# Hybrid streaming encoder step on 8 cores: stores and loads of x column by column inside the last down projection, weight casts with a marker for each half, and finish steps moved later

## The chip, the cores and the metric

The kernel runs on the 8 cores of one Trainium2 chip, each core on its own share of the streams (2 of the 16 prompt streams, 4 of the 32 sample streams). There is no traffic between cores. The metric is the device time of the slowest core in microseconds, as a median of runs.

## The reference

Two layers, each of them:

```python
x += 0.5 * down(silu(gate(norm(x))) * up(norm(x)))    # w1_*, D_MODEL 1024, D_FF 2816
z  = norm(x) @ w_in                                   # 3072 columns: qa ka va qb kb vb
oa = chunk-band attention (8 heads x 64, 9 chunks of 64 keys, relative bias, QK-norm)
ob = differential attention (4 heads, q/k halves of 64, values of 128, QK-norm, rotary, over the whole past)
x += concat(oa, norm(ob) * (1 - lam_init)) @ w_out
x += 0.5 * down(silu(gate(norm(x))) * up(norm(x)))    # w2_*
```

Outputs are x of the prompt (16 x 2048 rows) and sample streams (32 x 64 rows) and the new keys and values of both attention groups. Inputs and outputs are float32; the kernel multiplies in bfloat16.

## The kernel before

**Groups.** A core works through nine groups of tokens: four of 512 tokens for each of its two prompt streams (`i` is 0 to 3 within a stream, `seq` is 0 or 1), and one of 256 sample tokens. For each group both layers run: `ffn(l, 1)`, `mix(l)`, `ffn(l, 2)`. x of the group stays in SBUF transposed as `xT` (8 columns `dc` of 128 features x 512 tokens). `hT` is the same times the norm's gain, in bfloat16. `BIG` holds 22 tiles of 512 columns: the hidden activations `aT` of an ffn, the padded queries in mix, the staging `xstg` for the output.

**Order.** The program is one list of operations, each added with the tokens that it reads and writes; an operation waits for the last writer (and, if it writes, the readers) of its tokens, and each engine runs its operations in the order in which they were added. So a wait at the head of an engine's list holds everything behind it. DMAs are added to the list of the engine that issues them (SP, or POOL for stores).

**Ring of weights.** 168 weight tiles pass through a ring of 4 slots (`wring`, token `("w", s)`). In the first group every tile is loaded as float32 into borrowed parts of the key and value buffers (`first_load`) and cast into its slot (`first_cast`): the first half by DVE (L438), the second by ACT (L442) or, for w_in and w_out, by POOL (L440). Both halves write the same token. Half of the tiles are then written back in bfloat16 to `wsc` (`first_back`, L444, issued by SP), the others are cast again in the second group and written back then; every later use is a `fetch` (L450) from `wsc`. At the use of tile n the list gets: loads up to tile n+4, casts up to n+2, write-backs up to n+1, fetches up to n+2, in this order.

**ffn** (L542). 22 chunks `fc`: 8 matmuls for gate (L558), 8 for up (L562), then DVE gate x rstd (L568), ACT silu (L571), POOL x rstd (L573), DVE x up (L576). Chunk fc's last DVE step stands ahead of the next chunk's first one on DVE. A pair of chunks (`ft`) uses one gate and one up tile. Then the down projection in two halves of four columns (L582), `down_end` (L588) adds into `xT`, and `norm_feed` (L509, L511) squares and scales the column for the next norm; `norm_flush` (L498) sums the squares on PE.

**Between groups.** `store_y` (L650) transposes all of `xT` back (L657), copies to `xstg` (L661, L664) and stores 2 MB with one POOL DMA; then `load_x` (L629) transposes the next input, prefetched during the last ffn (L639), copies it into `xT` (L643, L646) and feeds the norm. The next gate matmul stands behind all of it.

**mix** (L692). Tables cosT and sinT are loaded by SP at its start, in each layer. A list of 32 jobs for a prompt group (q/k jobs and v jobs) runs as a software pipeline: in each step stages 5, 3, 2, 0, 1 of different jobs. Stage 0 (`Pst`) is the projection (L803 for q/k, L740 for v), stage 1 (`Bst`) the sums of squares (L819) and for group B the rotation matmul (L829), stage 2 (`Rst`) the DVE end of the rotation. The v jobs set the column of ones beside the values with a POOL memset (L751), ahead of ACT's copy of va (L753).

**Attention, prompt.** Group B: tiles of 256 keys, scores (L1032), exp on ACT (L1040), values (L1053), two tiles ahead. After a head's last tile `b_norm_m` (L975 to L979) and `b_combine` (L983) run: DVE adds both halves, squares and reduces (L985 to L991), ACT takes Ln and Exp of 128x4 values (L994, L996), DVE scales (L998). `o_transpose` (L1006) follows 6 tiles later (4 for i = 0). Group A's units follow (L1107, L1112, L1127), then w_out (L936).

## Time and profile before

| what | us |
|---|---|
| runs of the kernel | 7402.94, 7506.07, 7634.82 |
| median | 7506.07 |
| the profiled execution | 7388.71 |
| its span on the slowest core | 7387.7 (all cores 7348.1 to 7387.7) |
| its mean granted TensorE clock by core | 0.958 to 0.962 |

The profiled execution is one run of the program, on core 5. 1 us lies around its span. "Idle before" is the time for which an engine stood still ahead of an instruction, and the name behind the arrow is the instruction that ended the wait.

### The profile page before, as it was taken

The numbers are of one execution on the slowest core, as the hardware profiler recorded it, in microseconds if no ns is written. First come the engines' busy times: TensorE is split into PE (matmuls) and PEld (weight loads), VectorE is DVE, ScalarE is ACT, GpSimd is POOL, SyncE is SP. The second block draws the span as 40 slices with busy tenths as digits, with TensorE's granted clock in tenths as the row PEclk, the third lists the DMA queues.
The fourth block names the chain that finished last, engine by engine and source line by source line (L and its number), as shares of the span: only waits on it lengthen the run. The fifth ranks groups of instructions, "written<-read, shape, count | busy, mean of one in ns | idle before, by whom it ended". The sixth has DMA issues, their size and how long they took to land.

```text
span 7387.7 us, 115930 instructions; the slowest of 8 cores (7348.1 to 7387.7 us)
## 1 busy us (share of the span) xinstructions
PE 6565.3 (89%) x39776; PEld 3502.7 (47%) x39776; DVE 2890.4 (39%) x5156; ACT 2819.4 (38%) x4404; POOL 1504.9 (20%) x1757
## 2 busy tenths in 40 slices
PE   6787888888999998989898999999998989998888
PEld 2433334354444545454444444454545454456666
DVE  3535434343333334333434343333334333333433
ACT  3434335252333426162323233332516162433433
POOL 1212111211212121211212121212120211213332
PEclk9899999999999999999999999999999999998898
DMA  8799673736424242424433443434242424436877
GB/s 242 223 284 292 217 246 114 234 120 219 132 93 142 83 160 72 151 93 141 130 123 126 137 134 104 145 102 144 78 151 73 161 95 127 133 96 223 263 244 243
DMA packets 498890, 1162.09 MB, mean 157 GB/s; under 512 B 42000, under 2 KB 210704, under 8 KB 498320
## 3 DMA queue, kind: packets, MB, share of 16 engines
q1 hardware_dynamic: 480192, 1090.71, 46.7%
q0 software_dynamic: 18128, 63.97, 2.3%
q8 instruction: 335, 5.49, 0.3%
q14 instruction: 235, 1.93, 0.1%
HBM read 1004.57 MB, written 149.95 MB: 156 GB/s over the span
## 4 chain that ended last, share of the span: by engine, by line
PE 59%; DVE 11%; ACT 10%; issue 7%; DMA 6%; POOL 5%; SPq 2%; DVEq 0%; ACTq 0%; POOLq 0%
PE psb L582 14%; PE psb L558 11%; PE psb L562 11%; PE psb L803 6%; POOL tC L573 5%; PE psb L936 3%; PE psb L1032 3%; PE psb L1053 3%; DMA wring<-wsc 3%; ACT tA L571 2%; DVE tA L568 2%; PE psb L740 2%; SPq L270 2%; PE psb L1107 1%; ACT eT L1112 1%
## 5 line engine op out<-in xcount | busy, mean ns | idle before, releaser
L573 POOL TENSOR_TENSOR tC<-tA,rstdT 128x512 f32<-128x512 f32 (+1 forms) x792 | 954.6, 1205 | 4030.3 <-ACT tA L571 4030.3
L558 PE MATMUL psb<-hT,wring 128*128 128x512 bf16 (+1 forms) x6336 | 1446.9, 372 | 100.8 <-ACT wring L442 73.0
L562 PE MATMUL psb<-hT,wring 128*128 128x512 bf16 (+1 forms) x6336 | 1438.5, 370 | 70.8 <-DMA wring<-wsc 42.2
L582 PE MATMUL psb<-BIG,wring 128*128 128x512 bf16 (+1 forms) x6336 | 1325.2, 370 | 80.1 <-DVE BIG L576 43.1
L576 DVE TENSOR_TENSOR BIG<-psb,tC 128x512 bf16<-128x512 f32 (+1 forms) x792 | 524.3, 662 | 1809.8 <-POOL tC L573 1775.8
L571 ACT ACTIVATE tA<-tA 128x512 f32<-128x512 f32 (+1 forms) x792 | 480.9, 607 | 1945.2 <-DVE tA L568 1944.8
L558 PEld LDWEIGHTS psb<-hT,wring 128*128 128x128 bf16 x6336 | 621.1, 99 | 806.7 <-issue 162.1
L582 PEld LDWEIGHTS psb<-BIG,wring 128*128 128x128 bf16 x6336 | 619.8, 98 | 776.6 <-issue 119.0
L562 PEld LDWEIGHTS psb<-hT,wring 128*128 128x128 bf16 x6336 | 618.0, 98 | 771.0 <-issue 116.0
L568 DVE TENSOR_TENSOR tA<-psb,rstdT 128x512 f32<-128x512 f32 (+1 forms) x792 | 516.2, 652 | 182.2 <-ACT rstdT L524 162.7
L1040 ACT ACTIVATE eT<-psb 128x1024 bf16<-128x1024 f32 (+2 forms) x640 | 531.8, 894 | 95.3 <-PE psb L1032 58.8
L803 PE MATMUL psb<-hT,wring 128*128 128x512 bf16 (+1 forms) x2304 | 519.3, 371 | 5.0 <-ACT rstdT L519 4.6
L1032 PE MATMUL psb<-BIG,kbT 128*128 128x512 bf16 (+3 forms) x1280 | 372.1, 367 | 147.7 <-ACT eT L1040 127.8
L588 DVE SCALAR_TENSOR_TENSOR xT<-psb,xT 128x512 f32<-128x512 f32 (+1 forms) x288 | 186.7, 656 | 665.0 <-PE psb L582 664.7
L509 ACT ACTIVATE tq<-xT 128x512 bf16<-128x512 f32 (+1 forms) x216 | 130.9, 608 | 804.6 <-DVE xT L588 627.6
L1053 PE MATMUL psb<-vb,eT 128*128 128x129 bf16 x4352 | 371.6, 229 | 12.2 <-ACT eT L1040 10.9
L1053 PEld LDWEIGHTS psb<-vb,eT 128*128 128x128 bf16 x4352 | 298.3, 102 | 119.6 <-issue 33.3
L803 PEld LDWEIGHTS psb<-hT,wring 128*128 128x128 bf16 x2304 | 226.1, 99 | 228.1 <-issue 19.8
L740 PE MATMUL psb<-wring,hT 128*128 128x256 bf16 (+1 forms) x2304 | 300.1, 275 | 28.9 <-DVE tB L815 28.9
L1112 ACT ACTIVATE eT<-psb 128x1280 bf16<-128x1280 f32 (+4 forms) x256 | 278.5, 1103 | 104.2 <-PE psb L1107 100.9
L936 PE MATMUL psb<-BIG,wring 128*128 128x512 bf16 (+1 forms) x1152 | 275.8, 389 | 0.0
L740 PEld LDWEIGHTS psb<-wring,hT 128*128 128x128 bf16 (+1 forms) x2304 | 226.9, 100 | 89.6 <-issue 37.6
(197 smaller groups left out, 6399.0 us busy)
## 6 DMA issues: line engine op xcount, KB each, us to landing
wring<-wsc SPq DMA_DIRECT2D x1224, 512.0 KB, 3.9
wsc<-wring SPq DMA_DIRECT2D x160, 512.0 KB, 7.1
vb<-w_down SPq DMA_DIRECT2D x65, 512.0 KB, 10.0
vb<-w_gate SPq DMA_DIRECT2D x64, 512.0 KB, 8.7
vb<-w_up SPq DMA_DIRECT2D x64, 512.0 KB, 10.0
kbT<-w_up SPq DMA_DIRECT2D x100, 256.0 KB, 8.8
kbT<-w_gate SPq DMA_DIRECT2D x100, 256.0 KB, 6.5
kbT<-w_down SPq DMA_DIRECT2D x96, 256.0 KB, 8.8
```

Of the source, the lines that this page charges most:

```text
L558: P.add("pe", lambda kc=kc, bg=bg, wg=wg, fl=fl: nc.tensor.matmul(psb[bg][:, 0:T], wg[:, kc, fl * 128:(fl + 1) * 128], hT[:, kc, 0:T], sta ...
L562: P.add("pe", lambda kc=kc, bu=bu, wu=wu, fl=fl: nc.tensor.matmul(psb[bu][:, 0:T], wu[:, kc, fl * 128:(fl + 1) * 128], hT[:, kc, 0:T], sta ...
L568: P.add("dve", lambda bg=bg, ts=ts: nc.vector.tensor_tensor(out=tA[ts][:, 0:T], in0=psb[bg][:, 0:T], in1=rstdT[:, 0:T], op=ALU.mult), ["rs ...
L571: P.add("act", lambda ts=ts: nc.scalar.activation(out=tA[ts][:, 0:T], in_=tA[ts][:, 0:T], func=AF.Silu), [], [("t", ts, "A")])
L573: P.add("pool", lambda ts=ts: nc.gpsimd.tensor_tensor(out=tC[ts][:, 0:T], in0=tA[ts][:, 0:T], in1=rstdT[:, 0:T], op=ALU.mult), [("t", ts, ...
L576: P.add("dve", lambda bu=bu, ts=ts, fc=fc: nc.vector.tensor_tensor(out=aT[:, fc, 0:T], in0=psb[bu][:, 0:T], in1=tC[ts][:, 0:T], op=ALU.mul ...
L582: P.add("pe", lambda: nc.tensor.matmul(psb[ab][:, 0:T], wd[:, fl, dcl * 128:(dcl + 1) * 128], aT[:, fc, 0:T], start=(fc == 0), stop=(fc == ...
L740: P.add("pe", lambda kc=kc: nc.tensor.matmul(psb[b][0:bsz, 0:256], hT[:, kc, tb * bsz:(tb + 1) * bsz], wv[:, kc, :], start=(kc == 0), stop ...
L803: P.add("pe", lambda kc=kc: nc.tensor.matmul(psb[bz][:, 0:T], wv[:, kc, cl * 128:(cl + 1) * 128], hT[:, kc, 0:T], start=(kc == 0), stop=(k ...
L1032: P.add("pe", lambda j=j, u=u, q0=q0, o0=o0, w=w, r=r: nc.tensor.matmul(psall[:, o0:o0 + w], kbT[l][:, h, (j + u) * 128:(j + u + 1) * 128] ...
L1040: P.add("act", lambda: nc.scalar.activation(out=eP[:, es, lo:hi], in_=psall[:, bk * 512 + lo:bk * 512 + hi], func=AF.Exp, scale=0.125), [] ...
L1053: P.add("pe", lambda qt=qt, ob=ob, c=c, u=u: nc.tensor.matmul(psb[ob][:, (qt % 2) * 129:(qt % 2) * 129 + 129], eP[:, es, c:c + 128], vbt[l ...
```

## The change

It has seven parts. (1) The second half of a weight tile gets its own token `("w2", s)`, so ACT's or POOL's cast no longer waits for DVE's; readers wait for both. (2) The write-back to `wsc` is issued by ACT instead of SP. (3) At the end of a group the last down projection takes over the store and the load: `store_chunk` and `load_chunk` handle one column of 128 features; columns 0 to 3 are stored after the first tile of the second half, 0 to 2 loaded after the third and fourth, the others between the last columns' matmuls, 6 and 7 behind them. The output is staged in `hT` and in the first 8 tiles of `BIG`, with one 1 MB store for each half of the features. (4) cosT and sinT are loaded once a group, by POOL at the group's start. (5) The ones beside the values are set only in the first stream, and there for va only in i = 0 and 1. (6) For the q/k jobs of group B, but the first, stages 1, 2 and the row store come one step later, and a step's order is 6, 5, 4, 3, 0, 2, 1. (7) `b_combine` is split: its DVE part writes `tA`, its ACT part and the scaling (`b_finish`) come three tiles later; `o_transpose` follows 6 tiles after the head for every i.

In all matmuls that read a weight tile the token `("w2", ...)` is added to the reads; those lines are left out below.

```diff
@@ -437,21 +437,21 @@
                 if hf == 0:
                     P.add("dve", lambda: nc.vector.tensor_copy(out=dst, in_=buf), tk, [("w", s)])
                 elif name in ("in", "out"):
-                    P.add("pool", lambda: nc.gpsimd.tensor_copy(out=dst, in_=buf), tk, [("w", s)])
+                    P.add("pool", lambda: nc.gpsimd.tensor_copy(out=dst, in_=buf), tk, [("w2", s)])
                 else:
-                    P.add("act", lambda: nc.scalar.copy(out=dst, in_=buf), tk, [("w", s)])
+                    P.add("act", lambda: nc.scalar.copy(out=dst, in_=buf), tk, [("w2", s)])
...
-        dma("sp", wsc[tid][:, 0:nel], wring[:, s, 0:nel], [("w", s)], [("ws", tid)], ("wbk", s))
+        dma("act", wsc[tid][:, 0:nel], wring[:, s, 0:nel], [("w", s), ("w2", s)], [("ws", tid)], ("wbk", s))
...
-        dma("sp", wring[:, s, 0:nel], wsc[tid][:, 0:nel], [("ws", tid)], [("w", s)], ("w", s))
+        dma("sp", wring[:, s, 0:nel], wsc[tid][:, 0:nel], [("ws", tid)], [("w", s), ("w2", s)], ("w", s))
...
@@ -606,11 +606,27 @@
                 for fl in range(nfc):
                     for dcl in range(4):
                         down_mm(4 * t6 + fl, dcl, wd, fl, sd, (4 + dcl) if half == 0 else dcl)
+                if half == 1 and swap is not None:
+                    store_c, load_c = swap
+                    if t6 == 0:
+                        for dc in range(4):
+                            store_c(dc)
+                    for dc in ((), (), (0,), (1, 2))[t6]:
+                        load_c(dc)
             for dcl in range(4):
                 ab = (4 + dcl) if half == 0 else dcl
                 for fc, wd, fl, sd in held:
                     down_mm(fc, dcl, wd, fl, sd, ab)
                 down_end(half, dcl, ab)
+                if half == 1 and swap is not None:
+                    if dcl == 0:
+                        load_c(3)
+                    else:
+                        store_c(3 + dcl)
+                        load_c(3 + dcl)
+        if swap is not None:
+            store_c(7)
+            load_c(7)
 
...
+    def load_chunk(dc, T, b):
+        for tt in range(T // 128):
...
+        norm_flush()
+        if dc % 2 == 0:
+            P.add("act", lambda: nc.scalar.copy(out=xT[:, dc, 0:T], in_=psb[b][:, 0:T]),
+                  [], [PS(b), ("xT", dc)])
+        else:
+            P.add("dve", lambda: nc.vector.tensor_copy(out=xT[:, dc, 0:T], in_=psb[b][:, 0:T]),
+                  [], [PS(b), ("xT", dc)])
+        norm_feed(dc, T, 0, bank=7)
+
     def load_x(T):
+        for dc in range(8):
+            load_chunk(dc, T, rot())
+
+    ystg = [hT[:].rearrange("p c t -> p (c t)").bitcast(F32).rearrange("p (t d) -> p t d", t=4),
+            BIG[:, 0:4096].bitcast(F32).rearrange("p (t d) -> p t d", t=4)]
+    YTOK = [[("hT", c) for c in range(8)], Bk(0, 8)]
+
+    def store_chunk(dc, dst_rows, T, b):
         ntt = T // 128
-        for dc in range(8):
-            b = rot()
-            for tt in range(ntt):
...
-
-    def store_y(dst_rows, T):
-        ntt = T // 128
+        hf, d4 = dc // 4, dc % 4
         for tt in range(ntt):
-            for hf in range(2):
-                b = rot()
-                for d4 in range(4):
-                    dc = hf * 4 + d4
-                    P.add("pe", lambda dc=dc, d4=d4, tt=tt, b=b: nc.tensor.transpose(
-                        psb[b][:, d4 * 128:(d4 + 1) * 128], xT[:, dc, tt * 128:(tt + 1) * 128], ident[:]),
-                        [("xT", dc), "c"], [PS(b)])
-                if hf == 0:
-                    P.add("act", lambda tt=tt, hf=hf, b=b: nc.scalar.copy(
-                        out=xstg[:, tt, hf * 512:(hf + 1) * 512], in_=psb[b][:, :]), [], [PS(b)] + Bk(0, 16))
-                else:
-                    P.add("dve", lambda tt=tt, hf=hf, b=b: nc.vector.tensor_copy(
-                        out=xstg[:, tt, hf * 512:(hf + 1) * 512], in_=psb[b][:, :]), [], [PS(b)] + Bk(0, 16))
-        dma("pool", dst_rows.rearrange("(t p) d -> p t d", p=128), xstg[:, 0:ntt, :], Bk(0, 16), [], "yst")
+            P.add("pe", lambda tt=tt: nc.tensor.transpose(
+                psb[b][:, tt * 128:(tt + 1) * 128], xT[:, dc, tt * 128:(tt + 1) * 128], ident[:]),
+                [("xT", dc), "c"], [PS(b)])
+        out = ystg[hf][:, 0:ntt, d4 * 128:(d4 + 1) * 128]
+        in_ = psb[b][:, 0:T].rearrange("p (t f) -> p t f", t=ntt)
+        wt = [PS(b), ("yst", hf, d4)] + (YTOK[hf] if d4 == 0 else [])
+        if dc % 2 == 0:
+            P.add("act", lambda: nc.scalar.copy(out=out, in_=in_), [], wt)
+        else:
+            P.add("dve", lambda: nc.vector.tensor_copy(out=out, in_=in_), [], wt)
+        if d4 == 3:
+            dma("pool", dst_rows.rearrange("(t p) d -> p t d", p=128)[:, :, hf * 512:(hf + 1) * 512],
+                ystg[hf][:, 0:ntt, :], YTOK[hf] + [("yst", hf, c) for c in range(4)], [], "yst%d" % hf)
+
+    def make_swap(dst_rows, T, Tn):
+        bank = [0]
+
+        def nb():
+            bank[0] += 1
+            return 4 + bank[0] % 3
+        return (lambda dc: store_chunk(dc, dst_rows, T, nb())), (lambda dc: load_chunk(dc, Tn, nb()))
...
@@ -702,11 +731,6 @@
             i = grp["i"]
             sq_ = grp["seq"]
             tok0 = i * 512
-            dma("sp", cosT[:, 0:T], c_cosp[:, i * 512:(i + 1) * 512], [], ["cs"], "cs")
-            dma("sp", sinT[:, 0:T], c_sinp[:, i * 512:(i + 1) * 512], [], ["cs"], "cs")
-        else:
-            dma("sp", cosT[:, 0:T], c_coss[:, 0:T], [], ["cs"], "cs")
-            dma("sp", sinT[:, 0:T], c_sins[:, 0:T], [], ["cs"], "cs")
...
-                if half == 0:
+                if half == 0 and isP and sq_ == 0 and (isBv or i < 2):
                     P.add("pool", lambda: nc.gpsimd.memset(vfull[:, :, dh:dh + 1], 1.0), [], [tok])
                 if isP and not isBv and i < 3:
                     P.add("act", lambda: nc.scalar.activation(
...
-            st_ = {0: Pst, 1: Bst}
+            st_ = {0: Pst, 1 + late: Bst}
             if isB:
-                st_[2] = Rst
+                st_[2 + late] = Rst
             if need_rows:
-                st_[5 if kind == "kb" else 3] = Xst
+                st_[5 + late if kind == "kb" else 3] = Xst
...
         def add_q(kind, c):
-            jobs.append(qk_job(kind, c, nq[0] % 2))
+            late = 1 if kind[1] == "b" and not (kind == "qb" and c == 0) else 0
+            jobs.append(qk_job(kind, c, nq[0] % 2, late))
             nq[0] += 1
...
-        for step in range(nj + 5):
-            for k in (5, 3, 2, 0, 1):
+        for step in range(nj + 6):
+            for k in (6, 5, 4, 3, 0, 2, 1):
...
         def b_combine(h):
-            o4 = tB[0][:, 0:T].rearrange("p (a f) -> p a f", a=4)
+            ob_ = tA[h % 2]
+            OT = ("t", h % 2, "A")
             P.add("dve", lambda: nc.vector.tensor_tensor(
-                out=tB[0][:, 0:T], in0=tB[0][:, 0:T], in1=tB[1][:, 0:T], op=ALU.add),
-                [("t", 1, "B")], [("t", 0, "B")])
+                out=ob_[:, 0:T], in0=tB[0][:, 0:T], in1=tB[1][:, 0:T], op=ALU.add),
+                [("t", 0, "B"), ("t", 1, "B")], [OT])
             P.add("dve", lambda: nc.vector.tensor_tensor(
-                out=tC[0][:, 0:T], in0=tB[0][:, 0:T], in1=tB[0][:, 0:T], op=ALU.mult),
-                [("t", 0, "B")], [("t", 0, "C")])
+                out=tC[0][:, 0:T], in0=ob_[:, 0:T], in1=ob_[:, 0:T], op=ALU.mult),
+                [OT], [("t", 0, "C")])
             P.add("dve", lambda: nc.vector.reduce_sum(
                 out=rz[:, 8:12], in_=tC[0][:, 0:T].rearrange("p (a f) -> p a f", a=4), axis=mybir.AxisListType.X),
                 [("t", 0, "C")], [("rz", 2)])
+
+        def b_finish(h):
+            o4 = tA[h % 2][:, 0:T].rearrange("p (a f) -> p a f", a=4)
             P.add("act", lambda: nc.scalar.activation(out=rz[:, 12:16], in_=rz[:, 8:12], func=AF.Ln,
                                                       scale=1.0 / 128, bias=epsb[:, 0:1]), [("rz", 2), "c"], [("rz", 3)])
             P.add("act", lambda: nc.scalar.activation(out=rz[:, 12:16], in_=rz[:, 12:16], func=AF.Exp, scale=-0.5),
...
-                [("rz", 3), ("t", 0, "B")], [("hT", 4 + c) for c in range(4)])
+                [("rz", 3), ("t", h % 2, "A")], [("hT", 4 + c) for c in range(4)])
...
-                    lag = 4 if i == 0 else 6
-                    deferred.append([idx + lag, o_transpose, (1, h, 6 if lag <= nk // 2 else 4)])
+                    ph = -(-6 // (nk // 2))
+                    deferred.append([idx + 4, b_finish, (h,)])
+                    deferred.append([idx + 6, o_transpose, (1, h, 6 if ph % 2 else 4)])
...
+            if idx == 3:
+                flush(nt + 3)
...
     for gi_, grp in enumerate(groups):
         T = grp["T"]
-        load_x(T)
         if gi_ == 0:
+            load_x(T)
             setup_lam()
             setup_bias()
         nxt = groups[gi_ + 1] if gi_ + 1 < len(groups) else None
+        if grp["kind"] == "p":
+            i_ = grp["i"]
+            dma("pool", cosT[:, 0:T], c_cosp[:, i_ * 512:(i_ + 1) * 512], [], ["cs"], "cs")
+            dma("pool", sinT[:, 0:T], c_sinp[:, i_ * 512:(i_ + 1) * 512], [], ["cs"], "cs")
+        else:
+            dma("pool", cosT[:, 0:T], c_coss[:, 0:T], [], ["cs"], "cs")
+            dma("pool", sinT[:, 0:T], c_sins[:, 0:T], [], ["cs"], "cs")
         for l in range(NL):
             ffn(l, 1, T)
             mix(l, grp)
-            pre = None
+            pre = swap = None
             if l == NL - 1 and nxt is not None:
                 pre = prefetch_x(grp_rows(nxt, xp, xs), nxt["T"])
-            ffn(l, 2, T, pre=pre)
-        store_y(grp_rows(grp, yp, ys), T)
+                swap = make_swap(grp_rows(grp, yp, ys), T, nxt["T"])
+            ffn(l, 2, T, pre=pre, swap=swap)
+        if nxt is None:
+            for dc in range(8):
+                store_chunk(dc, grp_rows(grp, yp, ys), T, rot())
```

## Rows read from the trace of the kernel before

**Rows 1.** The page's first line
```profile
span 7387.7 us, 115930 instructions; the slowest of 8 cores (7348.1 to 7387.7 us)
```

**Rows 2.** Waits of PE, whole span: line waited for, us in total, times, longest
```profile
PE psb L1032 <- ACT eT L1040: 127.8, 131, 2.7
...
PE psb L1127 <- ACT eT L1112: 59.5, 69, 2.5
PE psb L819 <- ACT tq L806: 47.6, 52, 3.7
...
PE psb L562 <- DMA wring<-wsc: 42.2, 26, 3.5
...
PE psb L829 <- ACT tz L809: 21.2, 112, 0.2
```

**Rows 3.** Waits of ACT, whole span, same columns
```profile
ACT wring L442 <- DVE wring L438: 281.7, 92, 17.8
...
ACT rz L994 <- DVE rz L991: 132.0, 64, 3.7
...
ACT va L753 <- POOL va L751: 58.5, 23, 3.1
```

**Rows 4.** Windows, gate/up stretch of groups 1, 2, 3: PE, PEld, DVE, ACT, POOL, PEclk, DMA, GB/s
```profile
354.70:455.10 100.40, 81.16 (x354) 34.61 (x353) 42.01 (x72) 37.33 (x53) 25.32 (x20) 0.97 0.93 276
...
1245.20:1342.80 97.60, 81.47 (x354) 34.90 (x353) 35.78 (x61) 28.07 (x42) 26.56 (x21) 0.95 0.73 226
...
2943.50:3019.70 76.20, 76.20 (x354) 34.53 (x353) 26.34 (x41) 15.86 (x24) 24.62 (x20) 1.00 0.46 146
```

**Rows 5.** Timeline of ACT, then DVE, first group: start, us, instruction, idle before
```profile
112.07 1.05 ACT L442 CAST wring<-vb 128x1024 bf16<-128x1024 f32 x1 [2.89 <-DVE wring L438]
...
114.25 0.63 ACT L571 ACTIVATE tA<-tA 128x512 f32<-128x512 f32 x1
...
111.30 0.68 DVE L438 CAST wring<-vb 128x1024 bf16<-128x1024 f32 x1
...
112.77 0.68 DVE L568 TENSOR_TENSOR tA<-psb,rstdT 128x512 f32<-128x512 f32 x1
...
117.00 0.68 DVE L568 TENSOR_TENSOR tA<-psb,rstdT 128x512 f32<-128x512 f32 x1
```

**Rows 6.** Timeline of SP's issues, second group
```profile
975.31 0.34 SPq L270 DMA_DIRECT2D wring<-wsc  x1
988.32 0.34 SPq L270 DMA_DIRECT2D wsc<-wring  x1
...
990.85 0.34 SPq L270 DMA_DIRECT2D wring<-wsc  x1
```

**Rows 7.** Timeline at a head's end in group 3's attention B
```profile
2031.99 0.69 DVE L991 TENSOR_REDUCE rz<-tC 128x4 f32<-128x512 f32 x1
2032.78 0.30 ACT L994 ACTIVATE rz<-rz,epsb 128x4 f32<-128x4 f32 x1 [2.27 <-DVE rz L991]
...
2034.43 0.27 PE L1032 MATMUL psb<-BIG,kbT 128*128 128x256 bf16 x1 [2.73 <-ACT eT L1040]
```

**Rows 8.** Timeline of PE between groups 3 and 4: first transpose, first gate matmuls
```profile
2628.46 0.93 PE L657 MATMUL psb<-ident,xT 128*128 128x128 f32 x7
...
2644.31 1.89 PE L558 MATMUL psb<-hT,wring 128*128 128x512 bf16 x8
```

**Rows 9.** DMA issues: queue, count, KB each, median us to landing
```profile
yp<-BIG POOLq DMA_DIRECT2D x8, 2048.0 KB, 7.1
...
cosT<-c_cosp SPq DMA_DIRECT2D x16, 256.0 KB, 3.6
```

**Rows 10.** SP's write-backs in the first 300 us: ns min/median/max of the issue
```profile
L270 SPq DMA_DIRECT2D wsc<-wring x32: 326/375/2268, 28.9 to 285.4; - x32
```

**Rows 11.** Timeline of SP's issues at the first mix
```profile
208.47 0.53 SPq L270 DMA_DIRECT2D cosT<-c_cosp  x1
217.26 0.33 SPq L270 DMA_DIRECT2D sinT<-c_sinp  x1
```

38 lines of the change are left out of this document (15 added, 23 removed).

## The prediction

> **What bounds the kernel now.** I read the page first: the span is 7387.7 us [rows 1]. Then the windows of one gate/up stretch in three groups [rows 4]: in the third group PE is busy for all of its 76.20 us at full clock, with DMA at 0.46, so there nothing but PE sets the time. The same matmuls take 100.40 us in the first group and 97.60 us in the second. So PE is the bound, and what can be won is the time in which it stands still or is held up. The list of what PE waited for [rows 2] names the places: ACT's exp in both attentions (127.8 and 59.5 us), ACT's squares in the projection (47.6 us), fetched weights (42.2 us), the rotation's input (21.2 us). ACT is not full there, so I asked what ACT itself waited for [rows 3]: 281.7 us for DVE's half of a cast, 132.0 us for a reduction of DVE, 58.5 us for a POOL memset. Each of these is a wait at the head of ACT's list with work of others behind it. The timelines [rows 5 to 8] then give one case of each.
>
> **Part by part.**
>
> *Finish of a head (7).* Before, ACT's Ln waits 2.27 us for DVE's reduce, the next exps queue behind it, and PE's scores wait 2.73 us for them [rows 7]. There are 64 such waits (4 heads, 2 layers, 8 prompt groups), 132.0 us in all [rows 3], 2.06 us each. Moved three tiles later, the reduce is long done. ACT's own Ln and Exp stay (2032.78 to about 2033.3, some 0.5 us [rows 7]), and as ACT has little to spare in this loop I leave PE 0.3 us of each. Gain: 132 - 64 x 0.3 = 113 us. Bounds: at least half of it (66), if exps go on trailing; at most all 132. DVE does the same instructions as before, only L998 comes later, and o_transpose comes 2 tiles after that, so nobody waits for it. At i = 0 the heads are so short that DVE may become the bound; that is in the lower bound.
>
> *Projection (6, 5).* L829's 21.2 us [rows 2] are 112 waits for a tz made just before; a step more covers them. L819's 47.6 us are partly ACT held up by the memset: 58.5 us in 23 waits [rows 3], and the memset is gone from the third group on, while the late stage gives another 1.7 us or more of matmuls as cover. Waits of the group A jobs, which aren't moved, and of the third job's bank stay. I take 15 of the 47.6, together 36. Bounds 0 and 69. A bank and the tq, tz, tB buffers are held one step longer; the next q/k job that uses the same set comes 4 to 6 steps later, so nothing new waits. In the first group the projection runs beside saturated transfers; I count nothing more for it.
>
> *Store and load in the last down projection (3).* From the first transpose back to the first gate matmul it is 2644.31 - 2628.46 = 15.85 us [rows 8]. PE's own work in it stays: 64 transposes at 0.93 / 7 = 0.13 us, 8.5 us, and 8 norm matmuls at 1.89 / 8 = 0.24 us, 1.9 us. The remaining 5.4 us are waits for copies. Most are now hidden by the matmuls of columns 4 to 7; behind the last matmul stay the square of column 6 and the copies of 7. I leave 0.9 us: 4.5 x 8 swaps = 36 us; bounds 0 and 43. Two new waits: the scaled column 0 goes into `hT`, from which the first half of y is being stored. Between that store's issue and the first load lie two tiles of down matmuls: 32 matmuls at 0.24 us, 7.7 us. The whole 2 MB store landed in 7.1 us [rows 9], so 1 MB should be in time. Behind DVE's scaling would be the copies of columns 1 to 3, and PE would meet them only at column 4, some 5 us later. The second half's store, from `BIG`, is issued 1 to 2 us after the last matmul and must land before chunk 0's product, which comes about 10 us into the next gate/up; in time too.
>
> *Casts and write-backs (1, 2).* In the first group DVE casts from 111.30 to 112.77, 1.47 us, and ACT's casts only start at 112.07 behind the first of them; silu, whose input is ready at 112.77 + 0.68 = 113.45, starts at 114.25 [rows 5]. Untangled, ACT has its casts behind it by then: up to 0.7 us a pair of chunks, 11 pairs, 8 us a stretch. But DMA stands at 0.93 with 276 GB/s in that stretch [rows 4], so it can shrink by at most 7%, 7 us. I take 3 us x 4 = 12 us; bounds 0 and 28. In the second group only every second pair is cast and DMA is at 0.73. There SP waits from 975.31 to 988.32 for a write-back whose cast isn't done, and the fetch behind it goes out at 990.85 [rows 6], for PE too late (42.2 us at L562 alone [rows 2]). With the write-back on ACT the fetch goes as soon as its slot is free. What is left is DVE's chain: from L568 to L568 4.23 us in rows 5, less the 0.7 us of the tangle 3.53 us a chunk; four chunks and one pair's casts 4 x 3.53 + 1.47 = 15.6 us against PE's 4 x 76.20 / 22 = 13.9 us. That is 1.7 us for each of 5 converting pairs, 8.5 us late, so a stretch of about 85 us instead of 97.6: 12 x 4 less 1 each for the down side, 44 us. Bounds 0 and 4 x 21.4 = 86. The ACT issue of 168 write-backs costs about what SP's do, 0.375 us [rows 10]; ACT waits 2.89 us before each cast today [rows 5], which hides it. If that cover went, it would be 168 x 0.375 = 63 us.
>
> *Tables (4).* SP's second table waits for the first: 208.47 to 217.26 [rows 11], 8.8 us in which no weights are requested while transfers bound the group. Gone in two mixes, I take 5 us in all; bounds 0 and 17. Later groups have weights to spare. On POOL the same wait (3.6 us [rows 9]) stands behind y's second store and ahead of POOL's first product of the next ffn, which is not due for some 9 us.
>
> Here a rule of the Trainium skill bears: DMA: Bandwidth & Descriptors, section "Issuing engines are not separate DMA queues", says that transfers from all engines share the same 16 DMA engines and that a second issuer saves only issue time. The first group's row agrees (DMA at 0.93). By the rule alone parts 1 and 2 would give nothing but issue time; the wait in rows 6 is one of order in SP's list, which the rule does not speak of.
>
> **Sum.** 113 + 36 + 36 + 12 + 44 + 5 = 246 us. 7389 - 246 = 7143 us for an execution like the profiled one, 3.3% less. The three runs lie 0.2, 1.6 and 3.3% above the profiled one; the same three would give 7157, 7257 and 7382. A median may fall on the first or second, so I forecast between them: 7200.
>
> **Rivals.** (a) *Transfers bind both first groups*: parts 1, 2, 4 give nothing. For it: 0.93 in rows 4; against: 0.73 in the second group. 246 - 61 = 185 less, 7204 in the profiled state, 2.5%; still faster. 0.15. (b) *Stalls move on*: ACT and DVE trail at once elsewhere, since each is close to PE in attention, and half or less of parts 6 and 7 and of the swap is seen: 246 - 92 = 154, and with half of the casts' 56 gone 126 us, 1.7%, 7263. For it: 131 separate waits in the first row of rows 2, more than the 64 of the heads. Against: the longest are those of the heads. 0.18. (c) *Slower: ACT held by its write-backs.* An issue can take 2.27 us at the most [rows 10], when the transfers are backed up. If all 168 took that on ACT, 168 x 2.27 = 381 us would stand ahead of silu; with 246 won this is 135 us slower, 7524. It decides from 246 / 168 = 1.5 us an issue. Against it: the median is 0.375. 0.04. (d) *The store holds up the load*: y's first half lands late and DVE stands. It takes 4.5 + 5 us at each of 8 swaps to lose the 36 us again: 246 - 36 = 210, 7179. 0.05, within my forecast's range. Forecast: 0.58.
>
> **Range and chances.** A measurement of this kernel can tell about 2% from no change. The forecast (0.58), (a) and (d) are faster by over 2%: 0.78. (b) is within 2%: 0.18. (c) is slower, with more than 1.5 us an issue mostly by a little under 2%; half of it I count as over 2%: 0.02, and the other half as within: 0.20 in all. The range takes in the bounds (all upper ends give 132 + 69 + 43 + 28 + 86 + 17 = 375, 7014) only partly, and the spread of runs above: 7080 to 7340.
>
> **What would show it.** ACT's wait at the Ln line is nearly gone and PE's wait for exp falls from 127.8 below 60; no ACT cast waits for DVE; the second group's gate/up stretches are 83 to 88 us with no wait for `wsc`, the first group's still near 97 with DMA at 0.95 or more; from the last down matmul to the first gate matmul 5 us or less; the groups from the third on each 22 to 30 us shorter. Wrong would be: DVE waiting for the y store at L511; ACT's DMA issues over 1 us; PE's exp waits as many as before at other places.

## The result and the profile after

The changed kernel takes 7296.85 us as the median of its four runs (7049.52, 7544.17, 8272.15, 7047.71) against 7454.5 for the kernel before in the same job. In some executions of either kernel the cores of one die, or of both, show a lower granted clock for part of the time, and everything below is read from runs, cores and groups without it. Over such runs the ratio is 0.9529, with a 95% interval of 0.9488 to 0.957: 4.7% faster. The profiled execution of the changed kernel is one of these; its span is 7048.5 us, against 7387.7 [rows 1].

The page of the changed kernel, first its span, then the busy time of each engine:

```profile
span 7048.5 us, 116319 instructions; the slowest of 8 cores (6999.8 to 7048.5 us)
...
PE 6420.5 (91%) x39200; PEld 3486.8 (49%) x39776; DVE 2895.0 (41%) x5158; ACT 2817.6 (40%) x4406; POOL 1520.8 (22%) x1688
```

576 matmul records are missing from the changed kernel's trace (x39200 against x39776 weight loads), so its PE busy time is understated and I don't use its total. 339 us are gone. Where from? I cut PE's timeline at the first matmul of each stage, in both traces (slowest core against slowest core), and added up the stretches over the nine groups. The sample group's whole mix, projection and attention, counts as projection here:

| stage | before, us | after, us | difference |
|---|---|---|---|
| gate/up | 2837.0 | 2768.2 | -68.8 (group 1: -31.0, group 2: -43.0) |
| down, without the last of a group | 1137.8 | 1119.1 | -18.7 (group 1: -12.3) |
| last down with store and load | 471.4 | 429.3 | -42.1 |
| projection | 1385.8 | 1327.1 | -58.7 |
| attention B | 773.2 | 679.8 | -93.4 |
| attention A | 446.9 | 398.4 | -48.5 |
| out projection | 284.9 | 276.9 | -8.0 |

By group the difference is -73.6, -71.6, -37.6, -27.9, -29.6, -34.5, -38.9, -33.2 and, in the sample group, +8.7.

What PE waited for (line waited for, us in total, times, longest), the answer to [rows 2]:

```profile
PE psb L558 <- DVE wring L438: 60.4, 42, 6.6
PE psb L582 <- DVE BIG L576: 37.5, 33, 2.4
...
PE psb L1157 <- ACT eT L1142: 30.3, 69, 1.2
PE psb L1061 <- ACT eT L1069: 30.1, 89, 1.0
...
PE psb L764 <- DVE tB L839: 29.1, 17, 2.3
...
PE psb L1035 <- DVE tB L1004: 23.4, 20, 1.8
PE psb L1082 <- DVE rz L1000: 20.0, 19, 2.4
PE psb L843 <- ACT tq L830: 18.0, 29, 1.5
...
PE psb L562 <- DMA wring<-wsc: 12.3, 15, 3.2
```

L1061 is the scores' line, L1032 before: its wait for exp fell from 127.8 to 30.1 us, and the longest from 2.7 to 1.0. L1157 (L1127) went from 59.5 to 30.3, L843 (L819) from 47.6 to 18.0, L562's wait for a fetched tile from 42.2 to 12.3. Two rows are new near the top: L1035's wait for `tB` was 8.7 us, and L1082's for the reciprocal was not in the list. These are stalls that moved on, 35 us of them. The longest wait is now L558's for DVE's cast of the first half, 60.4 us; before it waited 73.0 us there for ACT's cast of the second. So PE's waits for casts changed their owner more than they shrank, and of its waits for fetched tiles 25.7 us are left in three lines, of 71.4.

What ACT waited for, the answer to [rows 3]:

```profile
ACT rz L1023 <- DVE rz L1017: 11.2, 4, 3.3
...
ACT wring L442 <- DVE wring L438: 3.2, 2, 1.6
```

The Ln at a head's end waits 4 times instead of 64, and the casts wait 3.2 us instead of 281.7.

Windows of one gate/up stretch in groups 1, 2 and 3, as in [rows 4]:

```profile
334.50:425.40 90.90, 78.73 (x347) 34.26 (x353) 41.05 (x71) 37.85 (x53) 25.41 (x20) 0.98 0.97 299
1149.00:1238.40 89.40, 82.42 (x348) 35.43 (x354) 36.60 (x62) 28.69 (x43) 26.62 (x21) 0.92 0.69 230
2746.50:2822.70 76.20, 75.83 (x347) 34.55 (x353) 26.35 (x41) 15.83 (x24) 24.97 (x20) 1.00 0.47 147
```

The third has not moved from 76.20. The first is 9.5 us shorter, and its transfers now run at 299 instead of 276 GB/s.

PE's timeline between groups 3 and 4, the answer to [rows 8] (start, duration, instruction, idle before):

```profile
2457.30 1.46 PE L582 MATMUL psb<-BIG,wring 128*128 128x512 bf16 x5
2458.59 0.60 PE L675 MATMUL psb<-ident,xT 128*128 128x128 f32 x4
...
2461.22 0.38 PE L498 MATMUL psb<-tz,onesb 128*128 128x512 bf16 x1 [0.46 <-ACT tz L509]
2461.44 0.81 PE L558 MATMUL psb<-hT,wring 128*128 128x512 bf16 x3
```

From the end of the last down matmul (about 2458.6) to the first gate matmul it is now 2.85 us.

### The profile page after: what moved, and what is told of

It reads as the page before. It is cut to its first block, busy times and chain, and to the rows that moved or that the text cites. A ratio compares the mean times of both kernels' runs of the same rounds, so it can differ in the third digit from the quotient of the medians.

```text
span 7048.5 us, 116319 instructions; the slowest of 8 cores (6999.8 to 7048.5 us)
## 1 busy us (share of the span) xinstructions
PE 6420.5 (91%) x39200; PEld 3486.8 (49%) x39776; DVE 2895.0 (41%) x5158; ACT 2817.6 (40%) x4406; POOL 1520.8 (22%) x1688
## 4 chain that ended last, share of the span: by engine, by line
PE 63%; DVE 8%; ACT 8%; issue 8%; DMA 5%; POOL 5%; SPq 2%; DVEq 0%; ACTq 0%; POOLq 0%
PE psb L582 15%; PE psb L562 11%; PE psb L558 11%; PE psb L827 6%; POOL tC L573 5%; PE psb L961 3%; PE psb L764 3%; DVE tA L568 3%; PE psb L1061 2%; ACT tA L571 2%; PE psb L1082 2%; SPq L270 2%; DMA wring<-wsc 2%; ACT eT L1069 2%; PE psb L1137 1%
## 5 line engine op out<-in xcount | busy, mean ns | idle before, releaser
L558 PE MATMUL psb<-hT,wring 128*128 128x512 bf16 (+1 forms) x6209 | 1425.5, 370 | 75.6 <-DVE wring L438 60.4
L562 PE MATMUL psb<-hT,wring 128*128 128x512 bf16 (+1 forms) x6239 | 1426.2, 370 | 49.5 <-DVE BIG L576 15.7
L582 PE MATMUL psb<-BIG,wring 128*128 128x512 bf16 (+1 forms) x6216 | 1327.8, 370 | 68.1 <-DVE BIG L576 37.5
L558 PEld LDWEIGHTS psb<-hT,wring 128*128 128x128 bf16 x6336 | 618.9, 98 | 769.1 <-issue 135.1
L562 PEld LDWEIGHTS psb<-hT,wring 128*128 128x128 bf16 x6336 | 617.3, 98 | 739.0 <-issue 95.2
L827 PE MATMUL psb<-hT,wring 128*128 128x512 bf16 (+1 forms) x2262 | 518.3, 373 | 8.0 <-ACT rstdT L519 4.7
L1061 PE MATMUL psb<-BIG,kbT 128*128 128x512 bf16 (+3 forms) x1176 | 331.7, 351 | 58.6 <-ACT eT L1069 30.1
L1082 PE MATMUL psb<-vb,eT 128*128 128x129 bf16 x4352 | 359.1, 224 | 23.1 <-DVE rz L1000 20.0
L1082 PEld LDWEIGHTS psb<-vb,eT 128*128 128x128 bf16 x4352 | 287.7, 100 | 125.5 <-issue 36.0
L764 PE MATMUL psb<-wring,hT 128*128 128x256 bf16 (+1 forms) x2304 | 280.2, 276 | 29.1 <-DVE tB L839 29.1
L511 DVE TENSOR_SCALAR hT<-xT,gx 128x512 bf16<-128x512 f32 (+1 forms) x432 | 223.9, 518 | 129.0 <-ACT xT L656 66.9
L764 PEld LDWEIGHTS psb<-wring,hT 128*128 128x128 bf16 (+1 forms) x2304 | 228.3, 100 | 85.6 <-issue 42.3
## 6 DMA issues: line engine op xcount, KB each, us to landing
vb<-w_gate SPq DMA_DIRECT2D x64, 512.0 KB, 11.3
```

Source lines behind the costliest of these rows:

```text
L558: P.add("pe", lambda kc=kc, bg=bg, wg=wg, fl=fl: nc.tensor.matmul(psb[bg][:, 0:T], wg[:, kc, fl * 128:(fl + 1) * 128], hT[:, kc, 0:T], sta ...
L562: P.add("pe", lambda kc=kc, bu=bu, wu=wu, fl=fl: nc.tensor.matmul(psb[bu][:, 0:T], wu[:, kc, fl * 128:(fl + 1) * 128], hT[:, kc, 0:T], sta ...
L582: P.add("pe", lambda: nc.tensor.matmul(psb[ab][:, 0:T], wd[:, fl, dcl * 128:(dcl + 1) * 128], aT[:, fc, 0:T], start=(fc == 0), stop=(fc == ...
L764: P.add("pe", lambda kc=kc: nc.tensor.matmul(psb[b][0:bsz, 0:256], hT[:, kc, tb * bsz:(tb + 1) * bsz], wv[:, kc, :], start=(kc == 0), stop ...
L827: P.add("pe", lambda kc=kc: nc.tensor.matmul(psb[bz][:, 0:T], wv[:, kc, cl * 128:(cl + 1) * 128], hT[:, kc, 0:T], start=(kc == 0), stop=(k ...
L1061: P.add("pe", lambda j=j, u=u, q0=q0, o0=o0, w=w, r=r: nc.tensor.matmul(psall[:, o0:o0 + w], kbT[l][:, h, (j + u) * 128:(j + u + 1) * 128] ...
```

## Experiments

Each of the first eight kernels is the kernel before with one part of the change (or two), so that a term of the sum can be read by itself. The last three start from the changed kernel. Spans are of the slowest core unless another is named, and stages are cut as in the table above. From group 3 on, a stretch that nothing in a kernel touches differs by 0 to 3 us between two executions. The first two groups, into which the weights stream as float32, are less steady: in the one execution of the kernel before, its eight cores take 913 to 927 us for group 1 and 845 to 865 for group 2, and core 5, with which the slowest cores are compared, has the longest group 2 of all. For these two groups I therefore also give the mean over cores (from the group's first gate matmul to the next group's, in us; least and most in brackets):

| kernel | cores | group 1 | difference | group 2 | difference |
|---|---|---|---|---|---|
| before | 0 to 7 | 920.0 (913 to 927) | | 855.7 (845 to 865) | |
| e_tokens: part 1 | 0 to 5 | 890.2 (889 to 893) | -29.7 | 852.0 (844 to 859) | -3.6 |
| e_wback: part 2 | 0 to 7 | 893.6 (885 to 899) | -26.4 | 831.6 (827 to 836) | -24.0 |
| e_cast: parts 1, 2 | 2 to 5 | 877.9 (861 to 894) | -42.0 | 812.8 (807 to 815) | -42.8 |
| changed | 0 to 7 | 849.8 (841 to 858) | -70.2 | 790.5 (782 to 799) | -65.1 |
| u_wback: changed, no part 2 | 0 to 7 | 851.2 (843 to 857) | -68.8 | 819.3 (811 to 830) | -36.4 |
| n_shadow | 0, 1, 4, 5 | 846.0 (838 to 854) | -74.0 | 794.6 (791 to 798) | -61.0 |
| e_swap: part 3 | 0 to 5 | 916.5 (908 to 923) | -3.5 | 848.0 (839 to 859) | -7.6 |
| e_tables: part 4 | 4 to 7 | 921.2 (915 to 927) | +1.3 | 851.2 (845 to 856) | -4.4 |

**e_heads: part 7 alone.**

```diff
-            o4 = tB[0][:, 0:T].rearrange("p (a f) -> p a f", a=4)
+            ob_ = tA[h % 2]                       # b_combine ends with the reduce
...
+        def b_finish(h):                          # Ln, Exp, scaling
...
-                    lag = 4 if i == 0 else 6
-                    deferred.append([idx + lag, o_transpose, (1, h, 6 if lag <= nk // 2 else 4)])
+                    deferred.append([idx + 4, b_finish, (h,)])
+                    deferred.append([idx + 6, o_transpose, (1, h, 6 if ph % 2 else 4)])
```

> The kernel before with only the finish of a head moved (b_finish three tiles later, o_transpose six tiles later). Theory P (the price in the prediction: the 132 us that ACT stood, less 0.3 us a head): 113 us less, a span near 7275. Theory C (a stall costs twice: the standing time, and after it matmuls at the lower granted clock): the sum over both attentions that the two traces show, 142 us less, near 7246, with a mean granted clock above 0.961 and PE's idle time shrinking by clearly less than the span. Theory I (the surplus comes from the parts acting together): 113 us or less here.

Measured: span 7246.3 us, 141.4 less than before. Attention B is 91.8 us shorter, attention A 51.5. One stretch of attention A in group 4, first in the kernel before, then in this one (length, busy time of PE, PEld, DVE, ACT, POOL, granted clock, DMA share, GB/s):

```profile
2897.03:2926.52 29.49, 23.77 (x311) 18.55 (x308) 10.11 (x27) 20.03 (x18) 0.00 (x0) 0.94 0.01 2
```

```profile
2838.59:2864.76 26.17, 22.11 (x309) 17.52 (x307) 10.02 (x27) 19.87 (x18) 0.00 (x0) 1.00 0.01 2
```

3.32 us less: 1.66 of them are idle time (5.72 to 4.06), and 1.66 are busy time. The same matmuls (the windows catch two more or less at their edges) run faster, at a granted clock of 1.00 instead of 0.94. Between the two levels, 1.2 and 2.4 GHz, a mean of 0.94 is about an eighth of the stretch at the lower one. This is not one stretch. All 32, summed in windows of PE for attention B and A:

| | before: length, busy, idle | e_heads: length, busy, idle |
|---|---|---|
| B | 773.2, 610.1, 163.2 | 681.4, 580.8, 100.7 |
| A | 446.7, 348.7, 98.0 | 395.3, 327.1, 68.2 |

So the waits gave 62.5 + 29.8 = 92 us and the busy time 29.3 + 21.6 = 51 us. That these 51 us are the clock can be checked from the trace's record of it: what PE's busy time in these stretches lost to the lower level (half of the busy time spent there) fell from 87 to 33 us, and the number of PE's stops hardly changed (432 and 436). Over all eight cores both attentions are 142 us shorter, the spread of cores about 3. Theory C holds. In the kernel before, ten of the 16 stretches of attention A ran at 0.94, two at 1.00 (28.3 us instead of 29.4), and the four of i = 0 at 0.75 or 0.76. In this kernel those four run at 0.88 to 0.90 and the twelve others at 0.99 or 1.00. It isn't the sum of idle time that decides, as the second of the two at 1.00 shows, with 6.03 us idle:

```profile
3311.33:3339.62 28.29, 22.26 (x309) 17.49 (x307) 10.12 (x27) 19.97 (x18) 0.00 (x0) 1.00 0.01 1
```

All twelve longer stretches of the kernel before have one wait of 2.0 us, some 4 us after their start. In ten of them a piece at the lower level begins 1.6 to 2.6 us behind it, in two none does. Here that wait is gone, the longest is 1.0 us, and no such piece follows. The Trainium skill's page "TensorE: Matmul & The Clock Gate", section "HAM oscillation — how this bites in real kernels", tells of a kernel in which PE's wait for data behind each short burst of matmuls sends its clock to the lower level every time; the direction agrees with these rows, though here the waits are for ACT and DVE and none is longer than 2.7 us.

What came back: L1010's wait for `tB` rose from 8.7 to 23.4 us, and 21.2 us of waits for the reciprocal are new.

```profile
PE psb L1036 <- ACT eT L1044: 34.2, 102, 1.0
...
PE psb L1132 <- ACT eT L1117: 30.1, 68, 1.0
PE psb L1010 <- DVE tB L979: 23.4, 20, 1.7
PE psb L1057 <- DVE rz L975: 21.2, 20, 2.4
```

**e_proj: parts 5 and 6.**

```diff
-                if half == 0:
+                if half == 0 and isP and sq_ == 0 and (isBv or i < 2):
...
-            st_ = {0: Pst, 1: Bst}
+            st_ = {0: Pst, 1 + late: Bst}
...
+            late = 1 if kind[1] == "b" and not (kind == "qb" and c == 0) else 0
...
-            for k in (5, 3, 2, 0, 1):
+            for k in (6, 5, 4, 3, 0, 2, 1):
```

> The kernel before with only the projection's parts: stages of group B's q/k jobs one step later, and the column of ones set only in the first stream. Theory P: 36 us less, near 7352. Theory C: what the two traces show for the projection stretches, 64 us less, near 7324. Theory I: 36 us or less, since the first group's transfers still bind it.

Measured, on cores 0 to 3: 7299.2 to 7310.8 us, where the kernel before has 7364.6 to 7382.5 on them. The projections of groups 2 to 8 are 9.4, 10.3, 5.7, 10.3, 10.4, 10.0 and 4.8 us shorter in the mean, 61 in all, the same on each core to 1 us; group 1's is 8 us shorter in the mean, but between two of the cores it differs by 11. Together 69 us, near theory C's 64. PE's waits on core 2:

```profile
PE psb L819 <- ACT tq L806: 18.9, 29, 2.2
...
PE psb L829 <- ACT tz L809: 2.9, 14, 0.5
```

47.6 and 21.2 before, so 47 us of listed waits went. The rest is not in that list: it lies in the busy time. The first projection stretch of group 2, in the kernel before and on core 2 of this one:

```profile
1100.76:1161.93 61.17, 54.84 (x318) 30.30 (x317) 34.53 (x51) 40.69 (x73) 9.60 (x24) 1.00 0.44 148
```

```profile
1098.86:1155.00 56.14, 53.05 (x317) 31.01 (x316) 35.14 (x51) 41.42 (x73) 9.64 (x24) 1.00 0.48 162
```

The same matmuls at the same clock keep PE busy for 1.8 us less. The timeline shows why. L821 and the matmul behind it, L829, before:

```profile
1120.14 0.38 PE L821 MATMUL psb<-lamt,blkb 128*128 128x512 bf16 x1
1120.71 0.38 PE L829 MATMUL psb<-tz,rpermb 128*128 128x512 bf16 x1 [0.19 <-ACT tz L809]
```

and here:

```profile
1118.50 0.38 PE L821 MATMUL psb<-lamt,blkb 128*128 128x512 bf16 x1
1118.72 0.38 PE L829 MATMUL psb<-tz,rpermb 128*128 128x512 bf16 x1
```

Without a wait, one such matmul starts 0.22 us behind the other, but each is recorded as 0.38 us long. So the first 0.16 us of every stop of PE count as busy: listed are 0.19 us, lost were 0.35. Over the projections of groups 1 to 8 PE's listed idle time fell from 107.1 us in 185 stops to 65.1 in 69. That is 42.0 us, and 116 stops fewer at 0.16 us are another 18.6, together 60.6; this core's projections are 60.4 us shorter.

**e_memset: part 5 without part 6.**

```diff
-                if half == 0:
+                if half == 0 and isP and sq_ == 0 and (isBv or i < 2):
```

> The kernel before with part 5 alone: the ones memset runs only in the first stream (two mixes), instead of in every mix. Part 6, the later stage of the q/k jobs, is left out. In the kernel with parts 5 and 6 the projection stretches of groups 1 to 7 got 5.6 to 11.9 us shorter, some 10 us each. Theory M (the memset holds ACT's list, PE waits behind it): ACT's wait for the memset (58.5 us in 23 waits) is gone from the third group on, and the projection stretches of groups 3 to 7 are 5 to 7 us shorter, 30 to 45 us in all; groups 1 and 2, where the memset stays, move by less than 1 us. Theory S (it was nearly all the later stage): the projection of groups 3 to 7 moves by less than 2 us each, span within 10 us of the kernel before. The numbers of groups 1 and 2 in the earlier run (-11.9, -8.0 with the memset still there) speak for S, the 58.5 us of waits for M.

Measured, on core 2 against core 5 of before: the projections of groups 3, 5, 6 and 7 are 4.8, 4.4, 4.7 and 4.3 us shorter, those of groups 2, 4 and 8 move by 0.3 at most. Group 1's got 8.6 longer and its down stretches 20 shorter; over cores 0 to 3 the whole group moved by 0.1 us. So neither theory alone. The memset is worth 2.2 to 2.4 us a mix in these four groups, 18 us in all. L819's wait falls from 47.6 to 28.2 us:

```profile
PE psb L819 <- ACT tq L806: 28.2, 37, 3.7
...
PE psb L829 <- ACT tz L809: 20.5, 109, 0.2
```

The later stage takes it on to 18.9 and removes L829's. It is the larger part, some 51 of the 69 us.

**e_swap: part 3.**

```diff
+                if half == 1 and swap is not None:
+                    store_c, load_c = swap
+                    if t6 == 0:
+                        for dc in range(4):
+                            store_c(dc)
+                    for dc in ((), (), (0,), (1, 2))[t6]:
+                        load_c(dc)
```

> The kernel before with only the store and load of x drawn into the last down projection. Priced 36 us; the traces show 42 us between the start of the last down projection and the next gate/up over eight groups. Near 7350. If the y store holds up DVE in the first two groups (10.8 us at the longest in the changed kernel) it is so here too, as the transfers are as dense; then the first two swaps bring less than 5 us each.

Measured: span 7354.8 us, 32.9 less. The last down stretches are 40.4 us shorter: 5.0 to 5.9 in groups 3 to 8, but 4.6 in group 2 and 1.4 in group 1. Over cores 0 to 5 it is 3.5 in group 1 and 7.6 in group 2, so only the first of the two expected short swaps is one; all eight together give 43 us.

**e_tables: part 4.**

```diff
-            dma("sp", cosT[:, 0:T], c_cosp[:, i * 512:(i + 1) * 512], [], ["cs"], "cs")
...
+            dma("pool", cosT[:, 0:T], c_cosp[:, i_ * 512:(i_ + 1) * 512], [], ["cs"], "cs")
```

> The kernel before with only cosT and sinT loaded once a group on POOL's list. Priced at 5 us, bounds 0 and 17: 7371 to 7389. If SP's 8.8 us without requests in the first two mixes mattered, the stretch from the first down projection to the projection is shorter by up to 8 us in each.

Measured, on cores 4 to 7: 7347.1 to 7373.5 us with a median of 7357.6, against 7366.8. The 9 us don't lie where the price sat: group 1 is 1.3 us longer in the mean and group 2 4.4 shorter, both inside the spread of cores, and group 8 is 5 us shorter. So the gap of 8.8 us in SP's list [rows 11] was real, but a gain of 5 us from closing it can't be told from none. That weights asked for sooner don't arrive sooner where transfers bind would explain it; no run shows it.

**e_tokens: part 1.**

```diff
-                    P.add("act", lambda: nc.scalar.copy(out=dst, in_=buf), tk, [("w", s)])
+                    P.add("act", lambda: nc.scalar.copy(out=dst, in_=buf), tk, [("w2", s)])
```

(and the same for POOL's cast, and `("w2", ...)` for each reader.)

> The kernel before with only the own token for each half of a tile. Theory P: DVE's chain gets up to 0.7 us shorter a pair of chunks; the first group's transfers (0.93 busy) allow 3 us a stretch, the second group keeps its late fetches, as SP still waits for the casts: 10 to 25 us in all, near 7370. Theory C': the order of lists, not the transfers, bound the first group: 4 x 7 us there and as much as 3 us a stretch in the second, 35 us or more, near 7350.

Measured: span 7350.9 us, 36.8 less. Group 1 lost 32.7 us (gate/up 28.4, down 12.4, and the projection gave 6.8 back), group 2 lost 5.5. The second gate/up stretch of group 1:

```profile
339.60:432.93 93.33, 77.95 (x354) 33.70 (x353) 41.06 (x71) 38.05 (x53) 25.39 (x20) 1.00 0.98 300
```

7.1 us less than in [rows 4], with DMA at 0.98 instead of 0.93 and 300 instead of 276 GB/s. Over cores 0 to 5 group 1 is 29.7 us shorter and group 2 3.6: theory C' for the first group, theory P for the second.

**e_wback: part 2.**

```diff
-        dma("sp", wsc[tid][:, 0:nel], wring[:, s, 0:nel], [("w", s)], [("ws", tid)], ("wbk", s))
+        dma("act", wsc[tid][:, 0:nel], wring[:, s, 0:nel], [("w", s)], [("ws", tid)], ("wbk", s))
```

> The kernel before with only the write-backs on ACT. Theory P: the second group's waits for fetched weights go, but casts stay tangled: 4 stretches to about 97 - 12 + 3 us each, 35 us less; nothing in the first group. If the issue cost on ACT mattered, silu would start later than before in the first group and its stretches grow.

Measured: span 7338.1 us, 49.6 less. Group 1 lost 25.0 us, 30.7 in its down stretches; group 2 lost 28.6, all in gate/up. Over all cores it is 26.4 and 24.0. For group 1 the expectation had nothing. SP's waits for a cast, first in the kernel before, then here:

```profile
SPq L114 <- ACT wring L442: 481.9, 83, 19.8
```

```profile
SPq L114 <- DVE wring L438: 282.8, 49, 38.3
```

**e_cast: parts 1 and 2 together.** Both of the edits above; the write-back then waits for both halves:

```diff
-        dma("sp", wsc[tid][:, 0:nel], wring[:, s, 0:nel], [("w", s)], [("ws", tid)], ("wbk", s))
+        dma("act", wsc[tid][:, 0:nel], wring[:, s, 0:nel], [("w", s), ("w2", s)], [("ws", tid)], ("wbk", s))
```

> The kernel before with both, the own tokens and the write-backs on ACT. The two traces show 71 us in the gate/up stretches of the first two groups and up to 20 us in the down projections: about 80 us less, near 7305. If the two parts are independent it is the sum of both single runs; if each alone leaves the other's wait in place, it is more than the sum.

Measured: the first two groups can be read on cores 2 to 5. On the slowest, core 3, they are 48.3 and 57.6 us shorter, 106 in all; in the mean 42.0 and 42.8, which is 85 and near the expected 80. The two single runs add up to 84. But the pair gives less than their sum in group 1 (42 against 30 + 26) and more in group 2 (43 against 4 + 24). In group 2 the parts need each other; in group 1 they share a limit.

**u_wback: the changed kernel without part 2.**

```diff
-        dma("act", wsc[tid][:, 0:nel], wring[:, s, 0:nel], [("w", s), ("w2", s)], [("ws", tid)], ("wbk", s))
+        dma("sp", wsc[tid][:, 0:nel], wring[:, s, 0:nel], [("w", s), ("w2", s)], [("ws", tid)], ("wbk", s))
```

> The changed kernel with part 2 alone undone: SP issues the write-backs of the cast weights again, ACT none. It tells whether the tokens of part 1 have made the order of SP's list harmless, since casts end sooner and a write-back at SP's head waits for less. Singly, part 2 gave 25.0 us in group 1 and 28.6 in group 2 on the kernel before. Theory O (order in SP's list is a cost of its own): the first two groups get 35 to 50 us longer than in the changed kernel, SP waits for casts ahead of fetches again, and PE waits for fetched weights; groups from the third on are the same to 2 us; span some 7090. Theory T (one cause, the tangle, seen twice): less than 10 us in both groups together, span within 10 us of the changed kernel's 7048.

Measured: span 7078.4 us, 29.9 more than the changed kernel. On the slowest core the first two groups are 8.4 and 36.8 us longer, with 42.6 in group 2's gate/up; over all cores it is 1.4 and 28.8, with 33.3 in group 2's gate/up. Its last gate/up stretch, first here, then in the changed kernel:

```profile
1581.65:1676.92 95.27, 82.74 (x354) 35.31 (x353) 36.29 (x62) 28.14 (x42) 26.62 (x21) 0.93 0.76 231
```

```profile
1545.01:1628.99 83.98, 78.48 (x347) 34.23 (x353) 34.52 (x59) 27.32 (x41) 25.38 (x20) 0.98 0.73 236
```

Of the 11.3 us, 7.0 are waits (12.5 against 5.5 us not busy); the rest is busy time, at a clock of 0.93 against 0.98. SP waits again:

```profile
SPq L114 <- DVE wring L438: 508.4, 95, 39.6
```

(236.5 us in the changed kernel), and PE's wait for fetched tiles at L562 is back at 47.2 us. Theory T, under 10 us, is out. Theory O holds for group 2 alone and with less than its 35 to 50 us: the price, 29 us, is paid there, at a DMA share of 0.76, and in group 1 the order costs nothing that can be told from the spread of cores. The Trainium skill's page "DMA: Bandwidth & Descriptors", section "Issuing engines are not separate DMA queues", speaks of issue time alone as what a second issuer saves. Group 1 of the changed kernel agrees with it. Group 2 doesn't, nor does group 1 of the kernel before, where part 2 alone gave 26 us: what is saved there is a wait in SP's list.

**n_shadow: the changed kernel with a pair's casts in the shadow of silu.** The ring's work of a pair is listed behind the silu of the pair's first chunk, so that DVE casts while it would wait for POOL.

```diff
-            sg = wload(l, "g%d" % f, ft)
-            su = wload(l, "u%d" % f, ft)
+            hold = []
+            sg = wload(l, "g%d" % f, ft, hold=hold)
+            su = wload(l, "u%d" % f, ft, hold=hold)
...
+                while hold:
+                    first_pass(hold.pop(0))
```

> The changed kernel, with the ring's work for a pair of chunks (loads, casts, write-backs, fetches) listed behind the silu of the pair's first chunk instead of ahead of the pair. DVE's casts then fill the 2.2 us in which it waits for POOL, so DVE's chain has no 1.47 us of casts: if that chain bounds the second group, its gate/up stretches go from 84 to 89 us towards 80, 20 to 30 us less than the changed kernel's 7048. In the first group it tells transfers from order: at 0.97 busy and 299 GB/s it gains little if transfers bind now, 5 us or more a stretch if the chain still does.

Measured: span 7195.8 us, of which groups 1 to 7 can be read. On the slowest core: group 1 +4.6, group 2 +2.1, groups 3 to 7 -3.7 to +5.0. Over cores 0, 1, 4 and 5 it is -3.8 in group 1 and +4.1 in group 2. Inside group 1 gate/up is 17.4 us shorter on the slowest core, and the down stretches 21.7 longer. Its last gate/up stretch and the down stretch behind it, first here, then in the changed kernel:

```profile
744.60:828.52 83.92, 78.65 (x348) 34.37 (x354) 43.30 (x73) 38.09 (x55) 28.84 (x21) 0.98 0.97 305
828.52:895.85 67.33, 53.90 (x243) 27.09 (x249) 21.95 (x38) 18.74 (x28) 2.95 (x3) 0.87 0.92 286
```

```profile
743.27:835.31 92.04, 78.45 (x347) 34.11 (x353) 41.31 (x72) 38.05 (x54) 25.40 (x20) 0.99 0.99 303
835.31:890.75 55.44, 50.10 (x242) 26.30 (x248) 22.43 (x40) 18.68 (x28) 3.35 (x3) 0.93 0.95 305
```

8.1 us won in the one, 11.9 lost in the other. So in group 1 the gate/up stretches of the changed kernel, taken alone, are still held by DVE's chain, yet nothing is won by freeing them: the weights come at about 300 GB/s in both kernels, and the time returns as a wait in the next stage. Outside attention DMA stands at 0.97 or more in nearly every stretch of group 1 by now, so the group is bound by transfers as a whole. In group 2 the expected 20 to 30 us did not come. DVE's chain is not what holds its stretches at 83 to 89 us, and no run shows what does.

**n_jobs: one more step of the same kind.** The changed kernel with DVE's rotation end (`Rst`) of the first group-B job listed two steps later than part 6 leaves it.

```diff
-                st_[2 + late] = Rst
+                st_[(4 if kind == "qb" and c == 0 else 2 + late)] = Rst
```

> The changed kernel with one more step of reordering in the projection: the rotation's last multiply-and-add of the first q/k job of a pair is listed at the earlier of the two steps, so that DVE has it done before the second job's work and PE does not meet it late. The changed kernel's trace shows PE at L764 waiting for DVE's tB of L839, 1.8 us in each of 16 mixes. Theory R (a wait of order on DVE): the wait is gone, each mix gets 1 to 2 us shorter, 15 to 29 us in all, span 7020 to 7035 in an execution like the profiled one of the changed kernel. Theory F (DVE is full in the projection and is late by the same amount at the next bank): the wait turns up at the next line of PE and the stage moves by less than 3 us in all. Against the kernel before the ratio is 0.949 by R and 0.953 by F.

The key of `st_` is the step after the job's start at which the work is listed; the expectation calls it "the earlier of the two steps", which is the wrong way round: it is listed at 4 instead of 2, so that the second job's first DVE step (L839), which frees the bank that PE waits for, comes ahead of it on DVE. The mechanism tested is the same: a wait that comes from the order of DVE's list.

Measured: 7016.80 and 7025.91 us, the kernel before in that job 7396.09, a ratio of 0.949. Against core 3 of the changed kernel, core 3 of this one has its projections 3.2 to 4.8 us shorter in every prompt group, and its span 27.5 us shorter (7027.8 to 7000.3). Over cores 0 to 3 the projections of groups 2 to 8 are 3.6 to 4.8 us shorter in the mean. L764 no longer waits for `tB` at all. Theory R holds; this version is some 0.4% ahead of the changed kernel, by this comparison of traces from two executions.

## Why the prediction came out as it did

The forecast was 7200 us, in a range of 7080 to 7340, faster by over 2%. The median of the four runs is 7296.85 and in the range, and that is luck: two of the four take 7047.71 and 7049.52 us, below the range's lower end, and the median lies halfway between the second of them and the run of 7544.17. The sharper test is the one that the prediction set itself: 246 us off an execution like the profiled one, 7143. The trace shows 339 off, 7048.5. The direction and the mechanisms held; the sizes were too small by 93 us. By terms, with what each measured alone, in means over cores (prompt groups):

| term | priced | alone | in the changed kernel |
|---|---|---|---|
| heads (7) | 113 | 142 | 146 |
| projection (5, 6) | 36 | 69 | 74 |
| swap (3) | 36 | 43 | 41 |
| group 1, casts and write-backs (1, 2) | 12 | 30 and 26, together 42 | 36 (gate/up 30, down 6) |
| group 2, the same | 44 | 4 and 24, together 43 | 37 (gate/up 38, down -1) |
| tables (4) | 5 | not told from 0 | not separable |

**Heads: too small, for a reason I had not in the sum.** The step "132 - 64 x 0.3 = 113" counts waits alone, and as a count of waits it was a little high: 92 us of idle time went. What it lacked is the clock. Before, PE ran ten of the twelve longer stretches of attention A at 0.94; without the gaps it runs them at 0.99 or 1.00, and over both attentions this gave another 51 us, which takes the gain above the upper bound of 132. The rows for it lay open in the trace of before: two stretches of attention A at 1.00 took 28.3 us, those at 0.94 took 29.4.

**Projection: half of what came, which is at or above the upper bound.** I took "15 of the 47.6"; 28.7 went. And 18.6 us more went in the first 0.16 us of each stop, which the profile counts as busy and no list of waits shows. The bound of 69 was the sum of two listed waits and had no room for it; "L829's 21.2 us [rows 2] are 112 waits" should have read 112 x 0.35 = 39 us. The memset was credited with part of the 15; it gave 18 us alone.

**Swap: right within 20%.** Priced at 4.5 for each of 8 swaps, 5.1 measured in the mean; the tail of 2.85 us meets "5 us or less". Transposes start 0.11 us apart where I had taken 0.93 / 7 = 0.13, so PE's own work was priced too high and the waits too low. In the changed kernel DVE's first scaling waits there for the store of y's first half, rival (d) in a small way:

```profile
874.11 0.49 DVE L511 TENSOR_SCALAR hT<-xT,gx 128x512 bf16<-128x512 f32 x1 [7.51 <-DMA yp<-hT]
...
1670.27 0.49 DVE L511 TENSOR_SCALAR hT<-xT,gx 128x512 bf16<-128x512 f32 x1 [10.80 <-DMA yp<-hT]
```

These are the only two such waits, and the prediction had named them as a sign of being wrong. In the other swaps the step "1 MB should be in time" held.

**Group 1: the step that failed.** "DMA stands at 0.93 with 276 GB/s in that stretch [rows 4], so it can shrink by at most 7%, 7 us" took one stretch for four, and a stretch for the group. The four gate/up stretches stood at 0.83, 0.93, 0.94 and 0.93, so their unused share was 40 us and not 28, and the down stretches, which I left out, stood at 0.87 to 0.93, another 23. Of these 63 us I took 12 and 36 to 42 came. Nor is the share a cap for one stretch: alone, the tokens made the gate/up stretches 32 us shorter, and n_shadow made them 53 shorter than before and gave the time back in the down stretches. The sign "still near 97" was wrong: the last three take 91 to 96 us, the first 113.5. The second half of that sign, DMA at 0.95 or more, was right in these three, and it is why nothing is left to win there: n_shadow's group 1 as a whole moved by less than the spread of cores.

**Group 2: right in size and in its first half.** Priced 44, measured 37 (43 on the slowest core); the stretches are 83.6, 89.3, 88.7 and 84.0 us there where 85 was expected. u_wback and e_cast show that the order in SP's list is what held it, as [rows 6] said, and that the tokens alone don't free it. The waits for fetched tiles are not gone, as the sign had it, but down from 71.4 to 25.7 us in all. "What is left is DVE's chain" was wrong: n_shadow took the casts out of the chain's way and the stretches got no shorter. What holds them stays open.

**Tables: not resolved.** The price of 5 us is smaller than the spread of cores in the two groups where it would show, and their means move by +1.3 and -4.4 us.

**The rivals.** (a) is refuted for the change, since the first two groups gave 73 us in gate/up and down; n_shadow shows it true of the changed kernel's group 1. (b) happened in part: 127 us went from the two waits for exp (127.8 to 30.1 and 59.5 to 30.3), and 35 came back as waits for DVE's `tB` and reciprocal. (c) didn't happen: ACT's write-back issues are

```profile
L270 ACTq DMA_DIRECT2D wsc<-wring x168: 326/326/400, 30.0 to 1673.5; - x168
```

0.326 us in the median and 0.400 at the most, far from the 1.5 us at which it would decide. The 2.27 us of [rows 10] are SP's; why some of its issues take so long, no run shows. The write-backs cost something else that nobody had priced: casts now wait until a write-back has landed, DVE for 54.8 us in 14 waits and ACT for 34.6 in 5, where the kernel before has no such wait. How much of it reaches PE is open.

Groups from the third on were forecast 22 to 30 us shorter each and are 28 to 39; the excess is the clock and the projection. The 8.7 us by which the sample group is longer are a difference of two cores: over all eight it takes 709.4 us before (697 to 722) and 705.5 after (698 to 718).

## What to carry to other kernels

Count a removed gap of PE three times: as listed idle time, with the part of each stop that the profile counts as busy (0.16 us here, the recorded length of a matmul less the distance of two starts), and by the granted clock of the stretch: where a stretch shows 0.94, look for one of the same kind at 1.00 and take the difference of their busy times into the sum. A semaphore token shared by two engines, or a slow instruction's wait at the head of a list that others share, costs more than its own duration and is found by asking what the waiting engine holds up. Where transfers bind a group, add up the unused DMA share of all the stretches that they feed, not of one; what is freed in one stretch can come back as a wait in the next. And where such a group's length differs between the cores of one execution, compare means over cores, not the slowest of each.

## What the runs showed of the hardware

- The granted clock fell behind waits no longer than 2.7 us, though not behind each: in ten of twelve stretches of attention A a piece at the lower level begins 1.6 to 2.6 us after a wait of 2.0 us, and in e_heads, where the longest wait is 1.0 us, there is none. In e_heads this was 51 of 143 us.
- Matmuls of 512 columns start 0.22 us apart and are recorded as 0.38 us long, so each stop of PE hides 0.16 us in its busy time: the same projection shows 54.84 and 53.05 us busy at a clock of 1.00, and 42.0 us of listed waits less made the projections 60.4 us shorter.
- A DMA share of 0.93 was not the ceiling. With requests in time the same stretch moved 299 to 300 GB/s at 0.97 to 0.98, against 276.
- The same 168 write-backs took SP 0.339 us each to issue in the median and 3.277 at the most (kernel before), ACT 0.326 and 0.400 (changed kernel), 0.327 and 0.582 (e_wback).
- Where transfers bind, the cores of one execution differ: 845 to 865 us for group 2 of the kernel before, where groups 3 to 7 differ by no more than 3 us.
